# Attention scores from rounded and low parts, with the low parts of queries and keys in the gates' buffer

## The reference

```python
h = rms_norm(x, norm_gain)
proj = h @ w_in        # qa ka va ga | qi ki wi | qb kb vb gb | ma mb
qa, ka, qb, kb = (apply_rope(rms_norm(t, gain)) for each)   # heads of 128
# branch A, 8 heads: the indexer's scores pick 64 keys for each query
s = einsum('bqhd,bqkhd->bqhk', qa_b, k_sel) * HEAD_DIM ** -0.5
p = softmax(where(valid, s, -inf));  oa = p @ v_sel
# branch B, 4 heads with two query/key maps each
s = einsum('bqhcd,bshcd->bhcqs', q_b, kb) * HEAD_DIM ** -0.5
p = softmax(where(causal, s, -inf))
ob = (p[:, :, 0] - lam * p[:, :, 1]) @ vb
ya = (oa * silu(ga)) @ w_o_a;  yb = (rms_norm(ob) * silu(gb)) @ w_o_b
x + (sigmoid(ma) * ya + sigmoid(mb) * yb) @ w_out
```

## Time and profile before

| | |
|---|---|
| median of 3 runs | 802.66 us (802.63 to 802.98) |
| profiled execution | 802.1 us |
| its span, first to last instruction | 800.3 us |
| TensorE busy | 796.5 us, 100% |
| VectorE busy | 470.4 us, 59% |
| ScalarE busy | 412.8 us, 52% |
| GpSimd busy | 48.0 us, 6% |
| granted TensorE clock | full, in every slice |
| DMA, mean | 191 GB/s |

### The profile page before, as it was taken

How to read it: one execution, slowest core, us unless ns; L and a number is a source line. 1 busy time by engine, 2 the same in 40 slices (tenths; PEclk the granted TensorE clock), 3 DMA queues, 4 the chain that set the end, 5 groups by cost and what they waited for, 6 DMA issues and landing times.

```text
span 800.3 us, 10778 instructions
## 1 busy us (share of the span) xinstructions
PE 796.5 (100%) x3764; PEld 667.5 (83%) x3764; DVE 470.4 (59%) x646; ACT 412.8 (52%) x640; POOL 48.0 (6%) x70
## 2 busy tenths in 40 slices
PE   9999999999999999999999999999999999999998
PEld 9998888888888888888888888888888888888887
DVE  7676666655567545568546455555455466665453
ACT  7584556555555444455455554555575444443431
POOL 4441000000000000000000000000000000000000
PEclk9999999999999999999999999999999999999999
DMA  9986665666676566666655555655665855555563
GB/s 311 307 262 212 184 188 173 180 197 185 183 207 186 172 174 183 179 185 189 180 154 167 172 170 160 181 162 163 177 183 184 291 186 185 191 187 191 187 193 123
DMA packets 81080, 152.90 MB, mean 191 GB/s; under 512 B 5136, under 2 KB 12944, under 8 KB 80784
## 3 DMA queue, kind: packets, MB, share of 16 engines
q1 hardware_dynamic: 80752, 152.06, 62.6%
q10 hardware_dynamic: 288, 0.30, 0.1%
HBM read 150.25 MB, written 2.10 MB: 190 GB/s over the span
## 4 chain that ended last, share of the span: by engine, by line
PE 100%; DVE 0%; issue 0%
PE ps L473 31%; PE ps L475 30%; PE ps L474 30%; PE ps L484 2%; PE ps L577 1%; PE ps L514 1%; PE ps L525 1%; PE ps L531 0%; PE ps L576 0%; PE ps L591 0%; PE ps L592 0%; PE ps L590 0%; PE ps L569 0%; PE ps L583 0%; PE ps L566 0%; PE ps L671 0%
## 5 line engine op out<-in xcount | busy, mean ns | idle before, releaser
L963 DVE TENSOR_TENSOR lo<-raw,hi 128x1024 fp32r<-128x1024 f32 (+2 forms) x279 | 336.3, 1209 | 311.2 <-ACT hi L723 310.2
L723 ACT ACTIVATE hi<-raw 128x1024 fp32r<-128x1024 f32 (+2 forms) x277 | 287.2, 1040 | 355.9 <-PE ps L475 341.8
L473 PE MATMUL ps<-hi,hT_hi 128*128 128x512 f32 (+2 forms) x952 | 373.9, 393 | 0.0
L475 PE MATMUL ps<-hi,hT_lo 128*128 128x512 f32 (+2 forms) x952 | 367.3, 386 | 0.0
L474 PE MATMUL ps<-lo,hT_hi 128*128 128x512 f32 (+2 forms) x952 | 366.7, 385 | 0.0
L475 PEld LDWEIGHTS ps<-hi,hT_lo 128*128 128x128 f32 x952 | 178.7, 188 | 35.8
L473 PEld LDWEIGHTS ps<-hi,hT_hi 128*128 128x128 f32 x952 | 178.7, 188 | 34.5 <-issue 1.3
L474 PEld LDWEIGHTS ps<-lo,hT_hi 128*128 128x128 f32 x952 | 178.9, 188 | 33.6
L473 PE MATMUL ps<-hi,ogT_hi 128*128 128x512 f32 x128 | 50.3, 393 | 0.0
L475 PE MATMUL ps<-hi,ogT_lo 128*128 128x512 f32 x128 | 49.9, 390 | 0.0
L474 PE MATMUL ps<-lo,ogT_hi 128*128 128x512 f32 x128 | 49.8, 389 | 0.0
(11 more groups left out here) (136 smaller groups left out, 422.5 us busy)
## 6 DMA issues: line engine op xcount, KB each, us to landing
raw<-in_w_in SPq DMA_DIRECT2D x192, 512.0 KB, 3.8
raw<-in_w_out SPq DMA_DIRECT2D x32, 512.0 KB, 4.3
raw<-in_w_o_a SPq DMA_DIRECT2D x16, 512.0 KB, 3.7
raw<-in_w_o_b SPq DMA_DIRECT2D x16, 512.0 KB, 3.7
raw<-in_w_in SPq DMA_DIRECT2D x13, 384.0 KB, 5.1
raw<-in_w_in SPq DMA_DIRECT2D x8, 336.0 KB, 6.2
x_own<-in_x SPq DMA_DIRECT2D x4, 512.0 KB, 6.2
g<-in_x SPq DMA_DIRECT2D x1, 2048.0 KB, 9.1
```

The lines of the kernel that those rows point to most:

```text
L473: mm(o, a_hi, w_hi[:, j], start=first and j == 0, stop=False)
L475: ins = mm(o, a_lo, w_hi[:, j], start=False, stop=j == 1 and (last or r in stop_rows))
L723: activation(hi[:, slot, :, 0:width], raw[:, slot, :, 0:width], ACT.Copy).then_inc(hi_ready, 1)
L963: tt(lo[:, slot, :, 0:width], raw[:, slot, :, 0:width], hi[:, slot, :, 0:width].bitcast(F32), ALU.subtract).then_inc(lo_ready, 1)
```

## The change

Scores are no longer one full-precision product. The transposed queries and keys are kept as a rounded part (`qk_hi`, in the place of `qkT`) and a low part (`qk_lo`, in the place of the merge gates `m`), and every score tile is the sum of three rounded products: hi by hi, hi by lo, lo by hi. ScalarE's copy of the transposes writes the rounded type, and VectorE subtracts it from the PSUM tile to get the low part, once for each of the eight chunks, at i = 7 of the chunk after it. The indexer's scores stay as they are. TensorE waits for the low parts of the chunk before at each `transpose_roped` (they read the PSUM banks that it writes), and for all eight before `index_scores(0)`. The chunks are computed in the order qa, qb, ka, kb, and blocks and gains follow, so that gate chunk j of `m` lies over the low parts of heads 2j and 2j + 1 of one branch.

```diff
         qk_at = place[0]
         qkT = sb("qkT", [P, 5 * 8, S])
+        qk_hi = sb("qk_hi", [P, 5 * 8, S], F32R, at=qk_at)
         x_own = sb("x_own", [P, RT, D], at=qk_at + 4 * 24 * S)
         ogT_hi = sb("ogT_hi", [P, KT, S], F32R, at=qk_at)
         ogT_lo = sb("ogT_lo", [P, KT, S], F32R, at=qk_at + 4 * KT * S)
-        QI, QA, KA, QB, KB = 0, 8, 16, 24, 32
+        QI, QA, QB, KA, KB = 0, 8, 16, 24, 32
         v_at = place[0]
         v = sb("v", [P, RT, 2 * A_W])
...
         m_at = place[0]
         m = sb("m", [P, RT, 2 * D])
+        m_r = sb("m_r", [P, RT, 2 * D], F32R, at=m_at)
         xt = sb("xt", [P, X_FRONT + KT * S], at=m_at)
         gainT, freq = xt[:, 0:KT], xt[:, KT:X_FRONT]
+
+        qk_lo = m_r[:, :, :].rearrange("p r n -> p (r n)").rearrange("p (b s) -> p b s", s=S)
         def x_tile(k):
             return xt[:, X_FRONT + k * S:X_FRONT + (k + 1) * S]
...
         x_squares, rstd_ready = sem("x_squares"), sem("rstd_ready")
         h_squares, r_h_ready, rope_done = sem("h_squares"), sem("r_h_ready"), sem("rope_done")
-        qk_transposed, qkT_ready = sem("qk_transposed"), sem("qkT_ready")
+        qk_transposed, qkT_ready, qk_lo_ready = sem("qk_transposed"), sem("qkT_ready"), sem("qk_lo_ready")
         idx_scores, idx_relu, idx_added = sem("idx_scores"), sem("idx_relu"), sem("idx_added")
...
                 if (c, i) in X_OWN_AFTER:
                     load_x_own(X_OWN_AFTER.index((c, i)))
-            rows = [(gains[:, j], row) for j, row in enumerate((a_q_gain, a_k_gain, b_q_gain, b_k_gain))]
+            rows = [(gains[:, j], row) for j, row in enumerate((a_q_gain, b_q_gain, a_k_gain, b_k_gain))]
             rows += [(lams[:, j], row) for j, row in enumerate((lambda_q1, lambda_k1, lambda_q2, lambda_k2))]
             rows += [(sub_gain[:, :], b_subln_gain)]
             for c, col in ((2, COL["qi"] + IDX_W[0] + IDX_W[1]),):
...
                         load_x_own(X_OWN_AFTER.index((c, i)))
                     for to, row in rows[i:i + 1] if c == 2 and i < CK - 1 else rows[i:] if c == 2 else ():
                         sp.dma_start(to, row[0].partition_broadcast(P)).then_inc(consts_landed, 16)
-            with sp.Fori(0, 2) as branch:
-                with sp.Fori(0, 4) as n:
-                    load_chunk(C_QK + branch * 4 + n, branch * COL["qb"] + n * CW)
+            for side in range(2):
+                with sp.Fori(0, 2) as branch:
+                    for n in range(2):
+                        load_chunk(branch * 2 + (C_QK + side * 4 + n), branch * COL["qb"] + (side * A_W + n * CW))
             for c, name in ((C_V, "va"), (C_V + 2, "vb"), (C_G, "ga"), (C_G + 2, "gb")):
                 with sp.Fori(0, 2) as n:
                     load_chunk(n + c, n * CW + COL[name])
...
                 pe.wait_ge(rope_done, n + 1)
                 if not isinstance(n, int) or n > 0:
                     pe.wait_ge(qkT_ready, n)
+                if not isinstance(n, int) or n > C_QK:
+                    pe.wait_ge(qk_lo_ready, n - C_QK)
                 for b in range(blocks):
                     for r in range(RT):
                         o = ps[:, T0 + b // 2, (b % 2) * S + r * P:(b % 2) * S + (r + 1) * P]
...
                 if four == 0:
                     pe.wait_ge(qkT_ready, C_V)
+                    pe.wait_ge(qk_lo_ready, C_V - C_QK)
                 else:
                     pe.wait_ge(idx_relu, 4 * four)
                 for pair in range(2):
...
             def qk_scores(q_block, k_block, bank):
-                o = ps[:, bank, :]
-                mm(o[:, 0:P], qkT[:, q_block, 0:P], qkT[:, k_block, 0:P], start=True, stop=True)
-                mm(o[:, P:P + S], qkT[:, q_block, P:S], qkT[:, k_block, :],
-                   start=True, stop=True).then_inc(scores, 1)
+                for q, keys, to in ((slice(0, P), slice(0, P), slice(0, P)), (slice(P, S), slice(0, S), slice(P, P + S))):
+                    q_hi, q_lo = (t[:, b, q] for t, b in ((qk_hi, q_block), (qk_lo, q_block - QA)))
+                    k_hi, k_lo = (t[:, b, keys] for t, b in ((qk_hi, k_block), (qk_lo, k_block - QA)))
+                    o = ps[:, bank, to]
+                    mm(o, q_hi, k_hi, start=True, stop=False)
+                    mm(o, q_hi, k_lo, start=False, stop=False)
+                    ins = mm(o, q_lo, k_hi, start=False, stop=True)
+                ins.then_inc(scores, 1)
             def transpose_probs(src, head):
...
             def qkT_out(n):
                 act.wait_ge(qk_transposed, n + 1)
-                activation(qkT[:, bass.ds((n - C_QK) * 4 + QA, 4), :],
+                activation(qk_hi[:, bass.ds((n - C_QK) * 4 + QA, 4), :],
                            ps[:, T0:T0 + 2, :].rearrange("p a (b s) -> p (a b) s", b=2),
                            ACT.Copy).then_inc(qkT_ready, 1)
...
                     rope_sum(IDX_BLOCKS[n] * P)
             nc.vector.memset(swapped[:, 0, 0:P], 0.0).then_inc(zeros_ready, 1)
+            def qk_lo_out(n):
+
+                dve.wait_ge(qkT_ready, n + 1)
+                tt(qk_lo[:, bass.ds((n - C_QK) * 4, 4), :],
+                   ps[:, T0:T0 + 2, :].rearrange("p a (b s) -> p (a b) s", b=2),
+                   qk_hi[:, bass.ds((n - C_QK) * 4 + QA, 4), :].bitcast(F32), ALU.subtract).then_inc(qk_lo_ready, 1)
+
             dve.wait_ge(x_landed[0], 16)
             ts(hT_hi[:, 0, :], x_tile(0), gainT[:, 0:1], None, ALU.mult).then_inc(x_hi_first, 1)
             dve.wait_ge(x_hi_first, 1)
...
                         index_rope(c - 1, i - start)
                     if c == C_QK + 1 and 1 <= i <= 3:
                         norm_rope(c - 1, 0, i - 1)
+                    if c == C_QK + 1 and i == 7:
+                        qk_lo_out(c - 1)
                     make_lo_ahead(c, i)
             before = wrote[0]
             for_each = 2 * (1 + 6)
...
                     for i in range(CK):
                         if 1 <= i <= 3:
                             norm_rope(c - 1, pair + turn, i - 1)
+                        if i == 7:
+                            qk_lo_out(c - 1)
                         make_lo_ahead(c, i)
             wrote[0] = before + 3 * for_each
...
                     u = c * CK + i
                     if c == C_V and 1 <= i <= 3:
                         norm_rope(c - 1, 3, i - 1)
+                    if c == C_V and i == 7:
+                        qk_lo_out(c - 1)
                     if C_INDEX <= c < C_INDEX + 4 and i % 2 == 0:
                         h = 4 * (c - C_INDEX) + i // 2
                         if h == 0:
```

## The result

The changed kernel takes 803.57 us (median of 22 runs, 803.1 to 804.7), the kernel before on the same chip 802.49 (22 runs, 802.05 to 802.98): ratio 1.0015, 95% interval 1.0009 to 1.0021. It is slower by 1.1 us or so. On another chip, beside two of the experiments, the pair was 803.75 against 802.04, ratio 1.0020 (1.0011 to 1.0029). The forecast was 804.1, 1.45 over the median that it started from; 1.1 and 1.7 lie on both sides of that, so the size holds.

The account below looks back on a forecast made before the run. TensorE's instruction stream was taken to bound the kernel. A 0.95 us stall before the index scores plus 0.5 for the score products, 1.45, on the 802.66 median gave 804.1 us, range 802.0 to 806.5.

Parts of the forecast that it names:

- TensorE's stream sets the time: Whole kernel: TensorE busy 796.5 of 800.3 us, so its added time counts and other engines' work is free unless TensorE waits.
- nothing in the rest of the kernel gives time back: Behind the index-score wait: every later stretch is bounded by TensorE, so the +0.95 us stays in the time.
- The narrow rounded product at 0.11, from its load: Score calls: each rounded 128-column product takes 0.11 us because its weight load is not hidden; three take 0.33.
- a line that said 0.067: Line through widths 512, 384 and 256, columns/2.4 GHz plus 0.013: would give 0.067 us for a 128-column rounded product.
- The 16 calls: Score products: 0.69 us a call against 0.65, +0.03 each, +0.5 us for all; bounds -1.5 to +5.9.
- The stall before the index scores: At index_scores(0), TensorE waits for the eighth subtraction, starting at 258.14 instead of 257.19: +0.95 us, once.
- Seven of eight subtractions at nothing: VectorE's first seven subtractions, 1.22 us each, fit its idle time before the next hi and cost TensorE nothing.
- The sum: Whole kernel: 0.95 for the stall plus 0.5 for the score products, 1.45 us, giving 804.1 us.
- B (passes): Rival, score calls: time follows passes, three instead of four, 0.49 us a call; 801.0 us with the stall; chance 0.04.
- A (cheap narrow products): Rival, score calls: the narrow products' weight load is hidden, -0.8 to -1.5 us, stall stays; 802.1 to 802.8; chance 0.12.
- C (the full-precision price): Rival, score calls: a narrow rounded product costs 0.22 us, +5.3 us on the forecast; 809.4 us; chance 0.12.
- D (no stall): Rival, before the index scores: the eighth subtraction goes ahead of the lo or starts earlier; 803.2 us; chance 0.06.

Follow-up runs that it names:

- e7b_double_seven: Changed kernel with the subtraction done twice for the first seven chunks, run again beside the changed kernel: 803.83 us, changed kernel 803.75, kernel before 802.04.
- e4_double_narrow: Changed kernel with the three 128-column score products done twice in every call: 808.41 us against 802.17 for the kernel before, ratio 1.0078.
- e9_narrow_at_256: Changed kernel with the three 128-column score products widened to 256 columns, the extra unread: 804.20 us against 802.16 for the kernel before, ratio 1.0026.
- e1_early_low: Changed kernel with the last key chunk's copy and eighth subtraction one turn earlier (i = 6): 802.70 us against 802.17 for the kernel before, ratio 1.0008.
- e3_low_alone: Changed kernel with low parts made but unused, each score tile one full-precision product over rounded parts: 803.37 us against 802.17 for the kernel before, ratio 1.0014.
- e8_double_eighth: Changed kernel with the subtraction done twice for the eighth chunk alone: 805.82 us against 802.16 for the kernel before, ratio 1.0048.
- both mixed versions: Changed kernel, queries 0 to 127 by full precision; eighth subtraction early 801.07 us (kernel before 802.16), or late 802.57 (kernel before 802.04).
- e2_scores_alone: Changed kernel without low parts, their subtractions and waits, rounded parts in all three products: 802.80 us against 802.17 for the kernel before, ratio 1.0010.
- e10_mixed_late: Changed kernel with queries 0 to 127 by full precision, eighth copy and subtraction at i = 7: 802.57 us against 802.04 for the kernel before, ratio 1.0003.

## Why the prediction was right

- **TensorE's stream sets the time.** Held in the main: 8.5 us more on VectorE off the path cost 0.1 (e7b_double_seven). But "nothing in the rest of the kernel gives time back" is not quite so. At the third and fifth head TensorE waits for ScalarE before it transposes the probabilities, and time added ahead of these two places is in part covered: 5.3 us more in the calls moved the end by 4.4 (e4_double_narrow). In the changed kernel itself this is worth under 0.1.
- **The narrow rounded product at 0.11, from its load.** There was no row of one, and the value was taken from the load of a rounded tile after transposes, against a line that said 0.067. Shown by e4_double_narrow (three for 0.335) and e9_narrow_at_256 (twice the columns for 0.026 a call). The call was forecast at 0.69 and is 0.69. The 16 calls were forecast at +0.5; followed to the eleventh product behind each they come to 0.42, because the two calls of a head of branch B together add little more than one of branch A.
- **The stall before the index scores.** Forecast 0.95, measured 1.05. The start of the subtraction was right to 0.01 once the trace's own shift of 0.2 is taken off. The release was not: 0.10 us passes between the end of VectorE's instruction and TensorE's next load, where I had taken 0.05. The added wait itself fills that difference. In the changed kernel it is an instruction of its own on TensorE's queue (L568), 51 ns long, that stands between the release and the load, while the wait of the earlier trace rows is carried by the load. e1_early_low takes the stall away and gets 1.05 of it back.
- **Seven of eight subtractions at nothing.** Shown by e7b_double_seven. VectorE's waits for hi are 7.4 us shorter (302.8 against 310.2 in the earlier trace rows), and no wait of TensorE on the new semaphore shows before the transposes.
- **The sum.** 1.45 forecast, 1.1 and 1.7 measured on two chips, 1.9 between the two spans. That the two terms sum so well is in part luck: the stall was 0.10 too low and the calls 0.08 too high, 1.47 in all. The traces add 0.19 ahead of the change, which the second trace has at -0.11, and 0.29 that was not forecast, 0.22 of it behind the transposes of the probabilities. There the changed kernel's twelve products after each take about 20 ns longer in sum than before. It is not chance of one execution, since both traces of the changed kernel have it. Nor does it go with one of the two parts: e3_low_alone (low parts, old products), e8_double_eighth and both mixed versions have it or more, and e1_early_low, e2_scores_alone, e4_double_narrow, e9_narrow_at_256 and both traces of the kernel with seven subtractions doubled don't. Its cause is open, and the change is not shown to be it.
- **The rivals.** B (passes) fell with e2_scores_alone, A (cheap narrow products) and C (the full-precision price) with e4_double_narrow. D (no stall) fell with the first trace.
- **The chances.** Same within 0.2% had 0.55, and the ratio is 1.0015 on one chip and 1.0020 on the other: at the edge, as the forecast of 1.45 under a bound of 1.6 said.

## What to carry to other kernels

Here a rounded (float32r) product of 128 columns costs what its weight load costs, not its columns; splitting a full-precision product of that width into three rounded ones makes it dearer, 0.33 us against 0.22, while at 256 columns it pays, 0.36 against 0.43, so choose by width. When an added step must end before a consumer on the bounding engine, look at the last one of the series, not at the typical one: seven were free and the eighth was 1.05 of some 1.75 us, and moving it one turn earlier cost nothing. A wait that TensorE already has later on can cover a part of what is added before it, so compare the whole stream and not only the changed place. An idle time that leaves the clock alone at 1.0 us can be followed by half the clock at 2.2.

## What the hardware showed that was not expected

- After 2.2 us without a product TensorE's granted clock was 0.50 for about 3.4 us (e8_double_eighth), which made the wait 1.7 us dearer in the two of five executions whose mean clock was under full; after 1.0 us (changed kernel) and 1.4 us (e10_mixed_late) it stayed at 1.00.
- A second wait in front of one load is not free on TensorE's queue. The wait for the low parts (L568) has a record of its own:

```profile
L568 PEldq EVENT_SEMAPHORE  x1: 51/51/51, 258.3 to 258.3; - x1
```

The load follows VectorE's end by 0.10 us here, and ScalarE's end by 0.05 where the load carries the only wait.
